# Encoder layer with mixture of experts on one core: attention tile by tile with the first tile's LayerNorm among its steps, the sample rows in quarters, and a first expert block written out ahead of sort and gates

## The reference

```python
x <- LN(alpha * x + g1 * Mix(x * (1 + s1) + b1))      # sh1, sc1, g1, sh2, sc2, g2 = silu(c) @ w_ada + b_ada
x <- LN(alpha * x + g2 * MoE(x * (1 + s2) + b2))      # alpha = 2 ** 0.25
# Mix: one input projection; attention A (4 heads, own chunk and 8 previous),
# attention B (8 heads, 2 kv heads, window 128, sinks), a convolution module; one output projection
logits = tok @ w_router + b_router
top_val, top_idx = lax.top_k(logits, 4)               # of 32 experts
gate = softmax(top_val)
hid = xb @ w_e_in[e] + b_e_in[e]                      # 1024 -> 2048
act = x_glu * sigmoid(1.702 * x_glu) * (x_lin + 1)    # clamped at 7
out = act @ w_e_out[e] + b_e_out[e]                   # 1024 -> 1024
```

## Time and profile before

| | |
|---|---|
| median of 3 executions | 1290.24 us (1288.34 to 1290.7) |
| the profiled execution's own time | 1290.84 us |
| its span in the trace | 1289.1 us, 30,824 instructions |
| mean granted TensorE clock | 0.917 |
| PE busy | 1026.4 us (80%) |
| DVE busy | 317.9 us (25%) |
| ACT busy | 183.3 us (14%) |
| POOL busy | 55.0 us (4%) |
| DMA | 455.05 MB, mean 353 GB/s |

### The profile page before, as it was taken

One profiled execution on the slowest core, in us unless ns is written; L12 is line 12 of the kernel. 1 busy time (PEld: TensorE's weight loads), 2 busy tenths in 40 slices (PEclk: granted clock), 3 DMA queues, 4 the chain that ended last, 5 costly groups with the idle time before them and its releaser, 6 DMA issues.

```text
span 1289.1 us, 30824 instructions
## 1 busy us (share of the span) xinstructions
PE 1026.4 (80%) x12341; PEld 487.2 (38%) x12342; DVE 317.9 (25%) x1042; ACT 183.3 (14%) x512; POOL 55.0 (4%) x137
## 2 busy tenths in 40 slices
PE   3799897498997877868698969997896897867872
PEld 2455653343443332423343433442343343332331
DVE  0295456712211211211121211121111111111215
ACT  0101332411111100101011101110111111110101
POOL 2900000000004000000000000000000000000000
PEclk9799899599998977988899989999898999888987
DMA  9987773279999999999799899089979979999993
GB/s 325 335 293 267 222 274 157 102 294 421 420 420 420 420 420 421 420 420 396 329 421 419 338 419 418 8 339 420 413 319 419 421 326 420 421 419 421 422 420 138
DMA packets 78075, 455.05 MB, mean 353 GB/s; under 512 B 9067, under 2 KB 16661, under 8 KB 28769
## 3 DMA queue, kind: packets, MB, share of 16 engines
q1 hardware_dynamic: 73840, 449.26, 86.0%
q10 hardware_dynamic: 4145, 4.41, 1.1%
HBM read 451.59 MB, written 2.61 MB: 352 GB/s over the span
## 4 chain that ended last, share of the span: by engine, by line
PE 38%; DMA 24%; SPq 22%; DVE 8%; issue 5%; ACT 2%; ACTq 0%; DVEq 0%
DMA w<-in_w_e_out 22%; PE bank L1677 15%; SPq L407 10%; PE bank L1705 8%; SPq L410 6%; PE bank L1658 3%; SPq L388 2%; PE comb L1637 2%; PE bank L1548 1%; DMA w<-in_ln_b 1%; SPq L374 1%; DMA w<-in_w_ada 1%; PE bank L1693 1%; PE bank L1670 1%; SPq L483 1%
## 5 line engine op out<-in xcount | busy, mean ns | idle before, releaser
L1677 PE MATMUL bank<-w,mt 128*32 128x512 f32 x3264 | 389.6, 622 | 45.8 <-DMA w<-in_w_e_in 45.8
L1705 PE MATMUL bank<-w,mt 128*32 128x256 f32 x3264 | 197.2, 387 | 45.8 <-DMA w<-in_w_e_out 31.8
L1677 PEld LDWEIGHTS bank<-w,mt 128*32 128x32 f32 x3264 | 96.4, 113 | 301.2 <-issue 215.8
L1224 DVE TENSOR_SCALAR mt<-bank 128x256 f32<-128x256 f32 x51 | 21.6, 424 | 718.6 <-PE bank L1677 718.6
L1705 PEld LDWEIGHTS bank<-w,mt 128*32 128x32 f32 x3264 | 98.7, 111 | 127.6 <-DMA w<-in_w_e_out 48.1
L1658 PE MATMUL bank<-pick,hb 128*128 128x32 bf16 x2448 | 80.2, 179 | 67.3 <-issue 64.2
L1658 PEld LDWEIGHTS bank<-pick,hb 128*128 128x128 bf16 x2448 | 75.4, 97 | 91.8 <-issue 91.8
L823 ACT ACTIVATE mt<-mt 128x256 f32<-128x256 f32 x51 | 21.3, 417 | 493.5 <-DVE mt L1224 493.5
L1637 PE MATMUL comb<-mt,gpickT 32*128 32x256 f32 x832 | 80.9, 462 | 0.5 <-ACT mt L830 0.5
L1659 PE MATMUL bank<-pick,hb 96*128 96x32 bf16 x408 | 72.5, 179 | 0.0
L1637 PEld LDWEIGHTS comb<-mt,gpickT 32*128 32x128 f32 x832 | 35.4, 199 | 49.2 <-issue 46.5
(11 more groups left out here) (335 smaller groups left out, 816.2 us busy)
## 6 DMA issues: line engine op xcount, KB each, us to landing
w<-in_w_e_in SPq DMA_DIRECT2D x256, 1024.0 KB, 26.0
w<-in_w_e_out SPq DMA_DIRECT2D x128, 1024.0 KB, 21.3
w<-in_w_ada SPq DMA_DIRECT2D x12, 2048.0 KB, 11.0
w<-in_w_in SPq DMA_DIRECT2D x3, 2048.0 KB, 21.9
w<-in_w_in SPq DMA_DIRECT2D x2, 1024.0 KB, 21.5
w<-in_w_out SPq DMA_DIRECT2D x4, 512.0 KB, 10.1
w<-in_w_out SPq DMA_DIRECT2D x2, 1024.0 KB, 12.3
w<-mod_rows SPq DMA_DIRECT2D x4, 512.0 KB, 6.6
```

The lines of the kernel that those rows point to most:

```text
L1677: ins = mm(quarter(bank[0][SLOTS * q:SLOTS * (q + 1), :], 0), xT[:, SLOTS * k:SLOTS * (k + 1)], quarter(slot[s], q), start=False, stop=(k ...
L1705: ins = mm(bank[0][SLOTS * q:SLOTS * (q + 1), 0:256], hid, slot[s][:, D * (k % 2) + 256 * q:D * (k % 2) + 256 * (q + 1)], start=False, sto ...
```

## The change

- **Attention by tile.** `ATT` has all six steps of tile 0 first, then the six of tile 1, then the sample. The pieces in `OP_AFTER` move accordingly, and the sample's output projection comes before the last piece of tile 1's.
- **Tile 0's LayerNorm among the steps.** `ln_half(0, ...)` and `ln_rest(0)` stand on DVE after steps 11, 12 and 13. The wait for `ld["brow"]` moves from behind attention to before attention's first maxima. What SP waits for before it issues these loads is unchanged.
- **Sample rows in quarters**: 32 rows of 1024 become 128 partitions of 256, in the load of x, in `sc2b` and the like, in LayerNorm (the statistics of the four quarters are joined by a product with `quad`, between `ln_stats` and `ln_spread`) and in the residuals. ACT stacks them again for the gather.
- **Two-pass LayerNorm**: (x - mean) * sc2b, then * 1/std + sh2b, both as one operation with three inputs; x stays as it was, and POOL normalises it later, behind the first nine blocks' second product.
- **Tile order** behind attention is `ORD` = 0, 2, 1. `choose` has nine operations.
- **First block of expert 0 written out** ahead of the loops (`block_work(..., opening=True)`). Its pick is made in `ranks`, as soon as the ranks are there. PE gathers for it as soon as `part3` is 5 and the pick is there; the sort, the visiting order and the gates run behind it. The sums are cleared by ACT during that block (`clear_sums`) rather than before it (`moe_zero`).
- **SP** loads expert 1's slots 2 to 7 after `part3` 5. At the end it loads the two gain rows first, with a semaphore of their own, and DVE starts with these alone. ACT's normalising in the second LayerNorm becomes pairs of DVE operations (`centred`, `scaled`).

The diff, cut:

```diff
-        ATT = [("A", t, j) for t in range(2) for j in range(2)] + [("B", t, i) for t in range(2) for i in range(4)] \
+        ATT = [(kind, t, i) for t in range(2) for kind, n in (("A", 2), ("B", 4)) for i in range(n)] \
             + [("SA", 2, 0), ("SB", 2, 0), ("SB", 2, 1)]
...
-        ORD = (0, 1, 2)
+        ORD = (0, 2, 1)
         OP_BANKS = ((0, 5), (4, 1))
-        OP_AFTER = {7: (0, 0, 3), 8: (0, 3, 6), 9: (0, 6, 9), 10: (0, 9, 12), 11: (0, 12, 14), 12: (0, 14, 16), 13: (1, 0, 4)}
+        OP_AFTER = {6: (0, 0, 3), 7: (0, 3, 6), 8: (0, 6, 9), 9: (0, 9, 12), 10: (0, 12, 14), 11: (0, 14, 16), 12: (1, 0, 4), 13: (1, 4, 8), 14: (1, 8, 12)}
...
             for dst, at in ((g1b, 2), (sc2b, 4), (sh2b, 3)):
                 sp.dma_start(dst[:, 0, :], mod_dram[0:1, D * at:D * (at + 1)].to_broadcast([P, D])).then_inc(ld["brow"], 16)
-                sp.dma_start(dst[0:32, 1, :], mod_dram[1:2, D * at:D * (at + 1)].to_broadcast([32, D])).then_inc(ld["brow"], 16)
+                quarters = bass.AP(tensor=mod_dram.tensor, offset=mod_dram.offset + 6 * D + D * at, ap=[[256, 4], [0, 32], [1, 256]])
+                sp.dma_start(dst[:, 1, 0:256], quarters).then_inc(ld["brow"], 16)
...
             load(1, 1, 0, 2)
             sp.wait_ge(op_done, 5)
             load(0, 0, 8, 12)
-            sp.wait_ge(part3, 3)
+            sp.wait_ge(part3, 5)
             load(1, 1, 2, 8)
+            sp.wait_ge(lg_done, 3)
             for rows, src in ((lng, ln_g), (lnb, ln_b)):
                 sp.dma_start(rows, src[0, 0:1, :].to_broadcast([P, D])).then_inc(ld_first, 16)
             sp.wait_ge(cum_ready, 2)
...
+            sp.dma_start(g2b, mod_dram[0:1, 5 * D:6 * D].to_broadcast([P, D])).then_inc(ld["gain"], 16)
+            sp.dma_start(g2q, quarters(mod_dram, 11 * D)).then_inc(ld["gain"], 16)
+            for rows, src in ((lng2, ln_g), (lnb2, ln_b)):
+                sp.dma_start(rows, src[0, 1:2, :].to_broadcast([P, D])).then_inc(ld["final"], 16)
+            for rows, src in ((lng2q, ln_g), (lnb2q, ln_b)):
+                sp.dma_start(rows, quarters(src, D)).then_inc(ld["final"], 16)
...
+                if s == 12:
+                    a.activation(warm[0:1, 0:1], warm[0:1, 1:2], ACT.Sqrt)
+                if s == 13:
+                    root(0, 1)
...
+            def ln_half(t, j):
+
+                c = slice(512 * j, 512 * (j + 1))
+                rows, row = XY[:, t, :], h2rows[t]
+                dve.wait_ge(op_done, j + 1 if t == 0 else (3, 5)[j])
+                link(v.tensor_tensor(row[:, c], bank[OP_BANKS[t][j]][:, :], g1b[:, 0, c], ALU.mult))
+                link(v.scalar_tensor_tensor(out=rows[:, c], in0=rows[:, c], scalar=ALPHA, in1=row[:, c], op0=ALU.mult, op1=ALU.add))
+                link(v.bn_stats(bnst[:, j, :], rows[:, c]))
...
+            def shifted(t, parts):
+
+                g = GROUP[t]
+                for rows, row, c in parts:
+                    ins = v.scalar_tensor_tensor(out=row, in0=rows, scalar=cstat[:, t, 0:1], in1=sc2b[:, g, c], op0=ALU.subtract, op1=ALU.mult)
+                link(ins)
+                inverse(t, ORD.index(t) + 1)
+                for rows, row, c in parts:
+                    v.scalar_tensor_tensor(out=row, in0=row, scalar=cstd[:, t:t + 1], in1=sh2b[:, g, c], op0=ALU.mult, op1=ALU.add).then_inc(h2_ready, 1)
...
+            dve.wait_ge(ld["brow"], 6 * 16)
             for s in logits_in(0):
                 maxima(s)
...
+                if s == 11:
+                    ln_half(0, 0)
+                elif s == 12:
+                    ln_half(0, 1)
+                elif s == 13:
+                    ln_rest(0)
...
-            dve.wait_ge(ld["brow"], 6 * 16)
...
+                                            in1=maskb[:, t, :], op0=ALU.add, op1=ALU.mult))
+                r = TS[t] if t < 2 else 96
+                return v.tensor_scalar(pick[0:r, t, :], iota[0:r, 0:SLOTS], rank[0:r, t, 0:1], None, ALU.is_equal)
...
-            ln_half(0, 0)
-            ln_half(0, 1)
-            ln_rest(0)
+            dve.wait_ge(b3_done, 1)
+            v.tensor_scalar(sel[:, 0, :], eye3[:, 0:1].to_broadcast([96, SLOTS]), 1.0, None, ALU.mult).then_inc(sel_ready, 1)
+            residual(0, 0)
             ln_half(1, 0)
-            residual(0, 0)
+            ln_sample_sums()
+            residual(0, 1)
+            ln_sample_rest()
             ln_half(1, 1)
             ln_rest(1)
-            residual(0, 1)
+            residual(2, 0)
             choose(0)
-            ln_half(2, 0)
-            ln_half(2, 1)
-            ln_rest(2)
-            residual(1, 0)
-            choose(1)
-            residual(2, 0)
-            residual(1, 1)
-            dve.wait_ge(rank_done, 1)
-            v.scalar_tensor_tensor(out=rank[:, 0:2, :], in0=bank[4][:, 128:128 + 2 * NE].rearrange("p (t e) -> p t e", t=2), scalar=1.0,
-                                   in1=maskf[:, 0:2, :], op0=ALU.add, op1=ALU.mult)
             choose(2)
             residual(2, 1)
-            dve.wait_ge(rank_done, 2)
-            link(v.scalar_tensor_tensor(out=rank[:, 2, :], in0=bank[4][:, 128 + 2 * NE:128 + 3 * NE], scalar=1.0,
-                                        in1=maskf[:, 2, :], op0=ALU.add, op1=ALU.mult))
+            residual(1, 0)
+            ranks(0)
+            ranks(2)
+            residual(1, 1)
+            choose(1)
+            ranks(1).then_inc(m["pick"], 1)
...
+            dve.wait_ge(ld["gain"], 2 * 16)
...
+            dve.wait_ge(ld["final"], 4 * 16)
+            centred(0, XY[:, 0, :], lng2)
+            inverse(0, 4)
+            scaled(0, XY[:, 0, :], lnb2)
...
-            out_proj(1, 4, 16)
             pe.wait_ge(o_copied, NATT)
             for k in range(DK):
                 for q in range(4):
                     ins = mm(bank[3][32 * q:32 * q + 32, 0:256], hT[:, k, SEQ:NTOK], w2v[:, k, 256 * q:256 * (q + 1)],
                              start=(k == 0), stop=(k == DK - 1))
             ins.then_inc(op_done, 1)
-
...
-            pe.wait_ge(part3, 3)
-            pe.wait_ge(moe_zero, 3)
...
+            pe.wait_ge(part3, 5)
             pe.wait_ge(b3_done, 1)
...
+                if opening:
+                    visiting_order()
+                else:
+                    combine(1)
+                    combine(2)
...
+            block_work(0, 1, turns, 1, 2, opening=True)
+            load_ends(pe, ends)
+            pe.wait_ge(y_zero, 2)
```

More of the change, by code:

```diff
@@ L733, in _, with root @@
             exps(1)
+            def root(t, n):
+                eng.wait_ge(ln_var, n)
+                a.activation(cstd[:, t:t + 1], cstat[:, t, 1:2], ACT.Sqrt).then_inc(ln_std, 1)
             for s in range(NATT):
@@ L778, in _, with gate_exp @@
+            def gate_exp(t):
+                eng.wait_ge(top_done, ORD.index(t) + 1)
+                a.activation(gate[:, t, :], lg[:, t, :], ACT.Exp, bias=rs[:, t:t + 1]).then_inc(gexp_done, 1)
             first_part(0)
-            root(1)
             second_part(0)
+            third_part(0)
+            root(2, 2)
+            copy_h2T(0)
+            sample_part(0)
+            root(1, 3)
+            stack_sample(0)
+            copy_h2T(2)
+            a.activation(warm[0:1, 0:1], warm[0:1, 1:2], ACT.Exp)
@@ L796, in _ @@
[L796 to L803 removed]
+            gate_exp(1)
@@ new lines, in ln_rest, with ln_sample_sums @@
+            def ln_rest(t):
+                link(v.bn_aggr(cstat[:, t, :], bnst[:, :, :]))
+                root(t)
+                shifted(t, [(XY[:, t, c], h2rows[t][:, c], c) for c in (slice(0, 512), slice(512, 1024))])
+            spread = rt[:, 0, 0:24].rearrange("p (q s) -> p q s", q=4)
+            def ln_sample_sums():
+                dve.wait_ge(op_done, 4)
+                dve.wait_ge(quad_done, 1)
+                row = h2rows[2]
+                link(v.tensor_tensor(row, bank[3][:, 0:256], g1b[:, 1, 0:256], ALU.mult))
+                link(v.scalar_tensor_tensor(out=x1q, in0=x1q, scalar=ALPHA, in1=row, op0=ALU.mult, op1=ALU.add))
+                link(v.bn_stats(bnst_s, x1q))
+                v.tensor_tensor(spread, bnst_s.unsqueeze(1).to_broadcast([P, 4, 6]), qmask[:, :].unsqueeze(2).to_broadcast([P, 4, 6]), ALU.mult)\
+                 .then_inc(ln_stats, 1)
@@ L1204, in moe @@
                     n2 = dve.snap(n + 2)
-                    first = nc.s_assert_within(dve.snap((n - lo) * SLOTS), 0, (NBLK - 1) * SLOTS, skip_runtime_bounds_check_because="an expert has at most nine blocks")
+                    first = nc.s_assert_within(dve.snap((n - origin) * SLOTS), 0, (NBLK - 1) * SLOTS, skip_runtime_bounds_check_because="an expert has at most nine blocks")
                     dve.wait_ge(cur_ready, e2)
```

627 lines of the change are left out of this document (303 added, 324 removed).

## The result

| | before | after |
|---|---|---|
| median | 1290.24 us (1288.34 to 1290.7, 5 executions) | 1303.17 us (1298.55 to 1305.66, 5 executions) |
| ratio | | 1.0101, 95% interval 1.0086 to 1.0116 |
| profiled execution | 1290.84, span 1289.1 | 1301.05, span 1299.3 |
| PE, DVE, ACT, POOL busy | 1026.4, 317.9, 183.3, 55.0 us | 1029.2, 312.0, 181.1, 65.0 us |

The change makes the kernel 12.9 us slower on the medians. The forecast was 1298 us, which is +7.5, with a range from 1288 to 1307. The profiled executions differ by 10.2 us. (The median of the kernel before is of five executions, not of three.)

The account below looks back on a forecast made before the run. The experts' weight stream was taken to set the time once started, its start waiting for TensorE. Terms 33.5 - 20.5 - 0.9 - 4.6 = +7.5 us on 1290.84 gave 1298.3, stated as 1298 us, range 1288 to 1307.

Parts of the forecast that it names:

- What bounds the kernel: From the experts' weight stream on, time is set; a microsecond at its start is a microsecond of the kernel.
- The moved wait: Attention's first maximum waits for the six rows until 182.1 us; attention 33.5 us later, between 30.5 and 37.
- Half clock after the long stop: TensorE in attention after idling some 34 us: another 6 us at half clock would add about 3, upper bound only.
- From the last projection to the first gather: Chain on DVE after attention: 18.1 us in place of 38.6, -20.5, between -17 and -23.
- The first two blocks: First gather to the stream's start, 23.15 us before: no combining in the first block, -0.9, between -2 and +0.5.
- the stream's start: Issue of the next weights behind expert 0's second block: from 278.8 to 290.9 us, +12.1.
- The end: Second LayerNorm: DVE starts behind the combining and its chain is shorter, -4.6, between -3 and -5.
- the split of the loads: At the kernel's end, gain rows first and alone let DVE start at about 1265.3 instead of 1268.35: -3.1.
- The pairs of DVE operations in place of ACT's: Second LayerNorm's 18.3 us DVE chain: ACT's normalising and its waits go, three-input pairs replace three passes, -1.5.
- The sum in the profiled execution: All terms over the whole kernel: +7.5 us, from 1290.84 to 1298.3 in the profiled execution.
- the short wait: Rival at SP's wait: state stores land early, attention only 11.4 later, sum -14.6, 1276 us; chance 0.07.
- the dearer case: Rival: longer half clock, slower quarter loads, smaller LayerNorm gain, late expert 1 slots; +16, 1303 to 1308 us; chance 0.17.

Follow-up runs that it names:

- k2_before_wait: Kernel before with only the `brow` wait moved ahead of attention's first maximum, plus bounded loads of expert 1's block range: 1319.63 us, ratio 1.0242.
- the control: Changed kernel with only expert 1's first and last block read by bounded loads: 1303.94 us, ratio 1.0113 to the kernel before.
- the experiment: Changed kernel with the `brow` wait at its first reader, DVE again awaiting all six rows at the end: 1268.89 us, against 1268.03 without that.

## Why the prediction was right, and where it was off

- **What bounds the kernel**: right. The stretch's extra microseconds come out at the end: 5.8 gave 5.2 in the time, 6.8 gave 7.1, 3.1 gave 3.5 (each against 1268.03, and each uncertain by some 4 us), and 34.4 at attention's start gave 35.9.
- **The moved wait**, 33.5: right in mechanism and nearly in size. The first exponential came at 183.53 against 149.28, 34.3 us later. That it met the rows within a microsecond is partly luck. The slowest landing (10.9 us) is that of the last load itself, so 182.1 is when the rows were in in the kernel before, with attention running. With attention waiting for them, the same loads are in at 178.3 (`k2_before_wait`). The new form, which I counted only as an upper bound of 3.3, costs about 4. The two, 2.8 less and 4 more, nearly cancel.
- **Half clock after the long stop**, costed at nothing with 3 us as a bound: it held in the profile of the changed kernel (5.7 us at half clock, 6.5 before), by chance. In the control it was 12.3, and from the first exponential to the last projection's end the control takes 71.8 us, 3.9 more than the kernel before and over the bound; the changed kernel's profile takes 0.9 more.
- **From the last projection to the first gather**, -20.5: right, 18.4 us in place of 38.6, so -20.2. The chain on DVE is the one that was added up. What stands for it in the old kernel is not only the operations moved away: putting the copies back late costs 6.8, LayerNorm 5.8, the pick 3.1. These need not add up, and what is left of the 20 (the sample in quarters, the shorter choice, clearing behind the first product) was not tried apart.
- **The first two blocks**, -0.9: wrong in sign. It took 24.0 us (270.68 to 294.72) in place of 23.15, +0.9. The step left out the clock: the first block's product ran 9.15 us, partly at half clock, where it had 7.44 before. In the trace of before the clock is at 1.00 again from 259.6, 4.0 us after the first gather, in that of after from 277.1, 6.4 us after it. It is tempting to put this down to the work that no longer stands ahead of the product, but that is not shown. `k2_before_wait` has the old blocks with all their work, and there the clock came back 6.1 us after the first gather (285.30), the product took 8.52 us and the stretch 24.2:

```profile
288.45 8.52 PE L1677 MATMUL bank<-w,mt 128*32 128x512 f32 x64
```

So 0.9 us is within what the clock does between one execution and the next.
- **So the stream's start**, +12.1: it was +15.9, that is 3.8 more: 0.7 in the wait, 1.0 between the first exponential (34.3 late) and the last projection's end (35.2 late), 0.3 in the chain on DVE and 1.8 in the blocks. All are from one profile of each kernel; the control's stream starts at 298.87, another 4.2 us later.
- **The end**, -4.6: it was -3.3 in the profile. The term that was mis-sized is the split of the loads, 3.1: it took DVE's start right behind the start of the last two products at 1265.03, while DVE started 2.2 us after the combining's start, which now ran at half clock (2.09 us for 16 products, 1.15 before), so that the profiles show 4.4 - 2.2 = 2.2, and the experiment 1.5. The pairs of DVE operations in place of ACT's gave 18.3 - 17.2 = 1.1 of the 1.5.
- **The sum in the profiled execution**: 15.9 - 3.3 = 12.6, while the spans differ by 10.2. The last combining starts only 13.5 us later (1277.44 against 1263.95), so 2.4 us were made up within the stream. Executions of the changed kernel differ by 7 us among themselves, and which 2.4 us these are stays open. On the medians it is 12.9.
- **The rivals**: the short wait did not happen, since the stores took 20.0 us. The Trainium skill's rule on turns between queues (DMA: Bandwidth & Descriptors, Queues, rings and completion order) would have made it likely; the runs show that 4 MB on the other queue did hold the stores for 10 us. Of the two others the dearer case was the nearer: 1303.17 is its lower edge. The clock and the quarter loads that it named were there; the 1.8 us in the first blocks, the largest deviation, it did not name.

## What to carry to other kernels

A wait belongs directly ahead of the first instruction that reads what it guards; ahead of a chain it costs what the whole chain could have done meanwhile, here 35.9 us against gains of 20. When a wait moves, look up in the trace of before when the awaited transfers land, and follow back what their issue waits for: that number was there, within a microsecond. When a sum is made of single microseconds around stops of TensorE, give the clock a term of its own with some microseconds to either side: here the same kernel spent 3.7 us at half clock in one execution and 9.8 in another.

## What was not expected of the hardware

- A source pattern with 4 in its outermost dimension made the last of six loads land 12.1 us after its issue (two profiles), in place of 7.8 for the same number of pieces with 128 outermost and 8.2 with 32 of 4 KB. The last form took 10.9 while attention ran.
- After a stop of 38 us TensorE ran at half clock for 5.7 us in one execution and 12.3 in another, after stops of 3.3 to 4.0 us for 3.5 to 9.8. The length of the stop does not show in it.
- The clock fell again behind a stop of 1.6 us in some executions (5.35 us for the second product) and not in others (3.66), with and without products that keep TensorE busy ahead.
- Two stores of 30 KB took 20 us behind 4 MB of loads on the other queue, and 10 us without them.
